# Stick attention in array halves: logits over 64 rows, values into 64 columns, issued in pairs

## What is computed

```python
def stick_breaking_attention(q, k, v):          # 8 heads of 64, blocks of 128 queries
    z = jnp.einsum('bqhd,bkhd->bhqk', q_blk, k) * scale
    mask = key_pos[None, :] < t[:, None]
    log_beta = jax.nn.log_sigmoid(z)
    log_1mb = jnp.where(mask, jax.nn.log_sigmoid(-z), 0.0)
    suffix = lax.cumsum(log_1mb, axis=3, reverse=True) - log_1mb
    att = jnp.where(mask, jnp.exp(log_beta + suffix), 0.0)
    return jnp.einsum('bhqk,bkhd->bqhd', att, v)
```

## Time and profile before

| | |
|---|---|
| median of three runs | 1359.57 us (1359.04 to 1359.7) |
| profiled execution | 1357.03 us |
| its span, first to last instruction | 1354.5 us |
| mean granted TensorE clock | 0.997 |
| TensorE matmuls | 1326.2 us, 98% of the span, 6205 records |
| VectorE | 787.3 us, 58% |
| ScalarE | 552.5 us, 41% |
| GpSimd | 615.3 us, 45% |

### The profile page before, as it was taken

How to read it: one execution, slowest core, us unless ns; L and a number is a source line. 1 busy time by engine, 2 the same in 40 slices (tenths; PEclk the granted TensorE clock), 3 DMA queues, 4 the chain that set the end, 5 groups by cost and what they waited for, 6 DMA issues and landing times.

```text
span 1354.5 us, 18086 instructions
## 1 busy us (share of the span) xinstructions
PE 1326.2 (98%) x6205; PEld 1077.5 (80%) x6205; DVE 787.3 (58%) x1097; ACT 552.5 (41%) x866; POOL 615.3 (45%) x299
## 2 busy tenths in 40 slices
PE   8999989999999999999999999999999999999997
PEld 7688867786778888888888777878788888888886
DVE  6798885633457777777533589886633333332222
ACT  6446686533252233223323254655433222332322
POOL 5598873432244444444444534222344444444441
PEclk9999999999999999999999999999999999999999
DMA  6123311221122232223322222111222222333221
GB/s 232 61 94 109 110 63 47 94 78 47 60 82 92 95 105 94 93 93 110 107 88 98 93 72 85 48 63 48 78 91 95 93 93 97 105 105 107 86 90 79
DMA packets 31876, 121.19 MB, mean 89 GB/s; under 512 B 3536, under 2 KB 3664, under 8 KB 31568
## 3 DMA queue, kind: packets, MB, share of 16 engines
q1 hardware_dynamic: 31536, 119.81, 26.2%
q10 hardware_dynamic: 288, 0.69, 0.2%
HBM read 118.40 MB, written 2.10 MB: 89 GB/s over the span
## 4 chain that ended last, share of the span: by engine, by line
PE 77%; issue 12%; POOL 5%; DVE 3%; ACT 2%; POOLq 0%; ACTq 0%; DVEq 0%
PE acc L1781 62%; POOL weights_low L644 4%; PE acc L1955 3%; PE aux L1890 2%; PE aux L2220 1%; PE aux L2199 1%; PE acc L2318 1%; PE aux L2209 1%; POOL conv L693 1%; PE acc L1923 1%; PE acc L1849 1%; PE aux L2053 1%; DVE a_low L1443 1%; DVE aux L1268 1%; ACT weights_high L722 1%
## 5 line engine op out<-in xcount | busy, mean ns | idle before, releaser
L644 POOL TENSOR_TENSOR weights_low<-weights_raw,weights_high 128x1024 fp32r<-128x1024 f32 (+1 forms) x204 | 529.2, 2594 | 706.5 <-ACT weights_high L722 705.5
L722 ACT CAST weights_high<-weights_raw 128x1024 fp32r<-128x1024 f32 (+1 forms) x202 | 222.0, 1099 | 497.1 <-PE acc L1781 459.6
L1781 PE MATMUL acc<-a_high,weights_high 128*128 128x512 f32 x944 | 376.2, 399 | 2.0 <-DVE a_low L1443 1.1
L1781 PE MATMUL acc<-a_high,weights_low 128*128 128x512 f32 x944 | 367.9, 390 | 0.0
L1781 PE MATMUL acc<-a_low,weights_high 128*128 128x512 f32 x944 | 367.6, 389 | 0.0
L1781 PEld LDWEIGHTS acc<-a_high,weights_high 128*128 128x128 f32 x944 | 177.4, 188 | 42.4 <-issue 3.3
L1781 PEld LDWEIGHTS acc<-a_high,weights_low 128*128 128x128 f32 x944 | 177.2, 188 | 37.5
L1781 PEld LDWEIGHTS acc<-a_low,weights_high 128*128 128x128 f32 x944 | 177.4, 188 | 37.1 <-issue 1.9
L1241 DVE TENSOR_TENSOR residual<-acc,residual 128x512 f32<-128x512 f32 (+1 forms) x63 | 43.3, 687 | 168.4 <-PE acc L1781 129.8
L1781 PE MATMUL acc<-h_high,weights_high 128*128 128x512 f32 x330 | 128.9, 391 | 0.0
L1781 PE MATMUL acc<-h_high,weights_low 128*128 128x512 f32 x330 | 128.4, 389 | 0.0
(11 more groups left out here) (402 smaller groups left out, 1985.6 us busy)
## 6 DMA issues: line engine op xcount, KB each, us to landing
weights_raw<-w SPq DMA_DIRECT2D x172, 512.0 KB, 3.2
weights_raw<-w SPq DMA_DIRECT2D x32, 704.0 KB, 4.0
residual<-xT SPq DMA_DIRECT2D x8, 256.0 KB, 6.9
out<-y_tok SPq DMA_DIRECT2D x4, 512.0 KB, 3.1
mem_raw<-memT SPq DMA_DIRECT2D x1, 1024.0 KB, 5.4
mem_tok<-mem SPq DMA_DIRECT2D x1, 1024.0 KB, 7.4
lru_weights<-blockdiag ACTq DMA_DIRECT2D x1, 512.0 KB, 3.4
sine<-positions SPq DMA_DIRECT2D x1, 256.0 KB, 7.3
```

Source lines behind the costliest of these rows:

```text
L644: g.tensor_tensor(weights_low[:, s, 0:cols], weights_raw[:, s, 0:cols], weights_high[:, s, 0:cols].bitcast(F32), ALU.subtract).then_inc(we ...
L722: a.copy(weights_high[:, s, 0:cols], weights_raw[:, s, 0:cols]).then_inc(weight_high, 1)
L1781: last = t_.matmul(acc[:, bank, 0:cols], w[:, s, wide], x_[:, k0 + k, 0:cols], start=start and k == opens and n == 0, stop=stop and k == c ...
```

## The change

Logits take only the 64 rows of their head, the values only the 64 columns of theirs, so that the two heads of a pair address different halves of the array. `k2` holds both heads, `v2` has no zeros, `k2_odd` and all clearing are gone. The logits of both heads are issued at the even step, head by head in turn, for qb > 0 in two parts of half the width; then both mask products. They wait for all sigmoids of the steps before. The values of both heads are issued three steps after the odd one, again in turn; `takeT` therefore has four buffers. The keys are written by one instruction and each `v2` block pair by one.

```diff
-        v2 = sb("v2", [P, QB, A_HEADS, P], where=s4)
+        v2 = sb("v2", [P, QB, A_HEADS, HALF], where=s4)
-        takeT = sb("takeT", [P, 2, T], where=s4)
+        takeT = sb("takeT", [P, 4, T], where=s4)
-        k2_odd = sb("k2_odd", [P, 4, T], where=s4a)
 # GpSimd
-            g.memset(k2[:], 0.0).then_inc(v2_clear, 1)
-            g.memset(k2_odd[:], 0.0).then_inc(v2_clear, 1)
             for b in range(QB):
-                g.memset(v2[:, b], 0.0).then_inc(v2_clear, 1)
                 low(CHUNK["in2"] // 2 + 1 + b // 2, b % 2, KB * P)
 # ScalarE
-                    if j >= 2:
-                        act.wait_ge(stick_heads, j - 1)
-                    a.copy(takeT[:, j % 2, 0:w], aux[2 + j % 2][:, 0:w]).then_inc(takenT_ready, 1)
+                    if j >= 4:
+                        act.wait_ge(stick_heads, j - 3)
+                    a.copy(takeT[:, j % 4, 0:w], aux[2 + j % 2][:, 0:w]).then_inc(takenT_ready, 1)
-                    act.wait_ge(v2_clear, 2 + QB)
-                    blocks = aux[5][:].rearrange("p (b f) -> p b f", f=P)
-                    for sub in range(2):
-                        a.copy(v2[:, :, 2 * j + sub, sub * HALF:(sub + 1) * HALF],
-                               blocks[:, :, sub * HALF:(sub + 1) * HALF]).then_inc(v2_out, 1)
+                    a.copy(v2[:, :, 2 * j:2 * j + 2], aux[5][:].rearrange("p (b s f) -> p b s f", s=2, f=HALF)
+                           ).then_inc(v2_out, 2)
 # VectorE, keys_out
-                for sub in range(2):
-                    rows = slice(sub * HALF, (sub + 1) * HALF)
-                    ins = v.tensor_tensor(k2_of[sub][rows, p], acc[rows, n % 2], row_factor[rows], ALU.mult)
...
+                v.tensor_tensor(k2[:, p], acc[:, n % 2], row_factor[:], ALU.mult).then_inc(tile_out[n % 2], 1)
 # TensorE, stick_step
-                    if step >= 2:
-                        pe.wait_ge(breaks, 2 * (step - 1))
-                    w = (qb + 1) * P
-                    t_.matmul(aux[sub][:, 0:w], q2[:, p, qb * P:(qb + 1) * P], k2_of[sub][:, p, 0:w],
-                              start=True, stop=False)
-                    t_.matmul(aux[sub][:, w - P:w], ident16[:], strict[:], start=False, stop=True
-                              ).then_inc(sticks, 1)
+                    if sub == 0:
+                        if step:
+                            pe.wait_ge(breaks, 2 * step)
+                        w = (qb + 1) * P
+                        cut = w if qb == 0 else w // 2
+                        for at in range(0, w, cut):
+                            for head in range(2):
+                                half = slice(head * HALF, (head + 1) * HALF)
+                                t_.matmul(aux[head][:, at:at + cut], q2[half, p, qb * P:(qb + 1) * P],
+                                          k2[half, p, at:at + cut], start=at == 0, stop=False)
+                        for head in range(2):
+                            t_.matmul(aux[head][:, w - P:w], ident16[:], strict[:], start=False, stop=True
+                                      ).then_inc(sticks, 1)
 # TensorE, stick_value
+                if sub == 0:
+                    return
                 pe.wait_ge(takenT_ready, j + 1)
-                if p and j % 8 == 0:
+                if p and j % 8 == 1:
                     pe.wait_ge(att_out, p)
                 for b in range(qb + 1):
-                    last = t_.matmul(aux[4][:, qb * P:(qb + 1) * P], v2[:, b, 2 * p + sub],
-                                     takeT[:, j % 2, b * P:(b + 1) * P],
-                                     start=sub == 0 and b == 0, stop=sub == 1 and b == qb)
-                last.then_inc(stick_heads, 1)
+                    for head in range(2):
+                        half = slice(head * HALF, (head + 1) * HALF)
+                        last = t_.matmul(aux[4][half, qb * P:(qb + 1) * P], v2[:, b, 2 * p + head],
+                                         takeT[:, (j - 1 + head) % 4, b * P:(b + 1) * P],
+                                         start=b == 0, stop=b == qb)
+                        if b == qb:
+                            last.then_inc(stick_heads, 1)
```

More of the change, by code:

```diff
@@ L224, in build @@
         left = sb("left", [P, T], where=s4)
-        takeT = sb("takeT", [P, 2, T], where=s4)
+        takeT = sb("takeT", [P, 4, T], where=s4)
         lru_in = sb("lru_in", [P, 4, TAPS_LRU + T], where=s4)
-        s4a = ExitStack()
-        k2_odd = sb("k2_odd", [P, 4, T], where=s4a)
-        s4a.close()
         y_low_late = sb("y_low_late", [P, 4, T], F32R, s4)
         y_lows = [y_low[:, n] for n in range(4)] + [y_low_late[:, n] for n in range(4)]
-        k2_of = (k2, k2_odd)
         s4.close()
@@ L352, in build @@
         v2_out = sem("v2_out")
-        v2_clear = sem("v2_clear")
         stick_scaled = sem("stick_scaled")
@@ L1592, in keys_out @@
             def keys_out(n, p):
-                if p == 0:
-                    dve.wait_ge(v2_clear, 2)
                 dve.wait_ge(chunk_done, CHUNK["in2"] + n + 1)
-                for sub in range(2):
-                    rows = slice(sub * HALF, (sub + 1) * HALF)
-                    ins = v.tensor_tensor(k2_of[sub][rows, p], acc[rows, n % 2], row_factor[rows], ALU.mult)
[L1600 to L1604, removed]
+                v.tensor_tensor(k2[:, p], acc[:, n % 2], row_factor[:], ALU.mult).then_inc(tile_out[n % 2], 1)
                 dve.wait_ge(tile_out[n % 2], TILE["in2"] // 2 + n // 2 + 1)
```

## The result

| | before | changed |
|---|---|---|
| median, same chip | 1359.77 us (6 runs, 1359.04 to 1363.41) | 1350.69 us (6 runs, 1350.11 to 1353.12) |
| profiled execution, span | 1357.03, 1354.5 us | 1351.5, 1349.6 us |
| mean granted TensorE clock | 0.997 | 0.994 |
| TensorE records | 6205 | 6253 |

The ratio is 0.9932 (95%: 0.9919 to 0.9945): 9.1 us faster, and the interval allows 7.5 to 11.0. A second measurement gave 1350.88 against 1358.96 us, ratio 0.9943 (0.993 to 0.9957), 8.1 us.

A forecast was written before the change was run, and what follows sets the result against it. TensorE was taken to bound the stage, its matmuls running one after the other. Overlap -12.3, in and out +11.2, waits -0.5 + 0.4 gave -1.2 us: 1358.4 us as median, 8-in-10 range 1351 to 1368.5.

The forecast's parts named there:

- overlap of the halves: Logits and values of the stick attention: the two heads' passes partly side by side, saving 11.3 to 13.3 us, taken as 12.3.
- in and out, 32 visits: TensorE going into and out of halves, twice a pair over 16 pairs: 10.7 to 11.7 us lost, taken as 11.2.
- second mask products and fewer gaps: Mask products behind the logits: now side by side, their number the same, so nothing was laid on them.
- TensorE's waits: First logits pairs' loss disappears in the wait for VectorE's scan, -0.5 us; waiting for ScalarE's sigmoids, 0 to 1.5, likely 0.4.
- the places: Logits and values of a pair: starts stay in program order, so N passes take N/2 + 1 places, not N/2.
- the 4.2 us that I kept as one end for the logits: Logits' weight loads of the two halves going one by one: 4.2 us saved in all, against 6.2 without that limit.
- the rival at 1366.5: Loads bind: a 64-column load costs as much as one of 128, values save nothing, +6.9 us; chance 0.14.
- The rival of cheap switches: Going in and out of halves costs half or nothing: -6.8 us, 1352.8, or wholly free -12.4, 1347.2; chance 0.27.
- What else moves: Outside the interludes: nothing ahead of step 1's scan is touched, its wait stays; dropped clearing and single key output bring zero.
- ScalarE's lead at even steps: Logits pairs wait for later sigmoids, step 28 tightest; rival that the lead is gone adds 3.6 us, 1362; chance 0.05.
- no overlap: Rival: the halves follow each other and going in and out is paid for nothing, +11.1 us, 1370.7; chance 0.13.

The follow-up runs named there:

- grouped: Changed kernel with both logits parts of head 0 issued first, then both of head 1: 1350.7 us, ratio 0.9942 to the kernel before.
- nocut: Changed kernel with the logits of a pair not cut in two parts: 1350.64 us, ratio 0.9944 to the kernel before.
- visit: Changed kernel with head 1's mask product moved between the logits parts for qb > 0: 1353.62 us, ratio 0.9961 to the kernel before.
- clear: Changed kernel with the clearing, two key outputs and two copies of `v2` put back: 1351.98 us, ratio 0.9951 to the kernel before.
- alone: Kernel before with logits and values in halves but unpaired, one head at a time at the old steps: 1370.31 us, ratio 1.0091.
- values_grouped: Changed kernel with all value key blocks of head 0 first, then all of head 1: 1354.52 us, ratio 0.9968 to the kernel before.

## Why the prediction was wrong

The direction was left open, with 0.33 on faster and 0.36 on no difference, and the time came out 7.7 us lower than forecast, 6.9 of them in the stage. The sum of the stage, predicted and as the runs have it:

| term | predicted | measured |
|---|---|---|
| overlap of the halves | -12.3 | -17.5 (half of all passes) |
| in and out, 32 visits | +11.2 | +10.1 (0.30 and 0.33 each) |
| second mask products and fewer gaps | 0 | -0.8 (worked out) |
| TensorE's waits | -0.5 + 0.4 | 0.0 (2.43 and 2.42) |
| sum | -1.2 | -8.2 (the stage gave 8.07) |

**The step that failed is the places.** The prediction said that starts stay in program order, and so N/2 + 1 places. It was an assumption about a resource of which no row of before tells, and I gave it no bound: the range of this term, 11.3 to 13.3, held only the question of the loads. The runs show that order isn't kept between the halves (grouped), that both begin together (the instants) and that no place is lost (nocut). Against the 12.3 of the forecast the overlap brought 8.65 + 8.9 - 12.3 = 5.2 us more: 4.2 by the places, since even with hidden loads I had only 13.3, and 1.0 because I had gone half way towards loads that bind. The Trainium skill ("TensorEngine Tiling (Array Packing)", Key Properties) says that different tiles can load weights and multiply in parallel. The records of this case agree, and I had read the page for the drain and not for that. The Trainium skill also says ("TensorE: Matmul & The Clock Gate", Part 3) that matmuls are strictly in program order in start and end. In grouped a matmul of head 1 began some 0.01 us after the first of head 0 with another of head 0 between them in the program. For independent halves the measurement decides.

**The loads don't bind.** The cut logits of qb = 1 took 0.43 us for eight passes, and load-bound they would have taken 0.88. The loads of both halves overlap, as the matmuls do. The value passes step at 0.054. So the 4.2 us that I kept as one end for the logits doesn't occur, and the rival at 1366.5 is false.

**In and out was right in kind, a little high.** The first records stand 0.09 us behind the end of the large pass before them (893.07 against 892.75 + 0.23), as I read from the earlier trace rows. 0.60 to 0.63 us a pair were measured for my 0.67 to 0.73. The rival of cheap switches, which came closest in time at 1352.8, is false as a mechanism: visit shows 0.30 for each. The time it gave, 2.1 us above the result, was nearly right by luck: switches at half price would have saved about as much as the overlap that I missed.

**The mask products** were put at nothing because their number is the same. The first logits of before leave 0.79 - 0.454 - 0.22 - 0.01 = 0.10 us for one. The first pair of the changed kernel (833.77 - 832.62 = 1.15) leaves, with 0.30 for in and out, 1.15 - 0.454 - 0.22 - 0.30 - 0.01 = 0.17 for two. So the second one costs 0.06 or 0.07, and 16 of them save about 0.6 us; 12 gaps at 0.01 are the rest of the -0.8.

**What else moves** was wrong in its sentence that the change touches nothing ahead of the scan of step 1: the keys' one output lies ahead of it and was worth about 0.6 us of the wait there (2.43 to 1.86, and clear has 2.5 again). The 0.5 us of loss that the wait was to hide didn't exist: TensorE reached the transposes 0.10 us earlier after the first mark than before. But 0.55 came back as a new wait of step 33's transposes for `take`: counted from the first mark, VectorE had that `take` 7.2 us earlier than before, and TensorE reached its place 8.1 us earlier. ScalarE's lead at even steps held: no matmul waits for `stay` in the changed kernel, and only loads do, for 0.5 us. At step 28, too, no wait of a matmul is seen.

**Of the rivals,** no overlap is false. The 1370.31 us of alone, so near to the 1370.7 that I had given this rival, is no test of its price: alone goes in and out for each head by itself, 15.8 us in all, where the rival had 11.2 for 32 visits. But it shows that without overlap the halves only cost: the overlap is what pays for them.

## What to carry to other kernels

Two half-array fp32 matmuls whose operands lie in different halves take the time of one, loads included, if they stand next to each other in the instruction stream or with at most one other between; without a partner, a half only costs. A change of the array's shape costs about 0.3 us in and out here, so with 0.055 us saved a pass it pays from about six passes of 128 columns on, and work in halves should be gathered. When TensorE gets faster in a stage that three engines share, look first for what is just behind the longest wait: removing 1.07 us of matmul time or a 1.86 us wait brought nothing measurable here. And look at what runs beside the instruction that is waited for: the scan here takes 2.56 us beside GpSimd's subtraction and 0.42 away from it.

## What the runs showed of the hardware

- Two halves of the array run side by side in both passes of an fp32 matmul and in the loads: 0.054 us a pass against 0.111, in halves by rows and by columns alike, starts some 0.01 us apart.
- The halves don't keep program order between them, but the look-ahead is short (grouped, values_grouped): two matmuls in a row for one half cost nothing, three 0.26 us and four 0.49.
- Leaving and entering costs 0.30 us (rows) and 0.33 us (columns), 0.44 for both side by side.
- VectorE's instructions are stretched beside GpSimd's subtraction of 128x1024: a scan of 128x128 from 0.42 to 2.56 us, a product of 128x512 from 0.69 to 2.83.
- A load of 64 columns is recorded with 137 ns, one of 128 with 192.
- The clock fell to 0.50 for 3.4 us in some executions and not in others after like stretches of idleness, at a cost of 2.63 us for the two of one profile.
